# A two-block transformer kernel on one core: the layer mixers' projections issued in grains between recurrence and attention units, and GpSimd's remainder in four parts

## What is computed

```
h = h + 0.5 * swiglu(rmsnorm_2(h, ffn1_norm[l]), ...)
z = rmsnorm_2(h, mix_norm[l]) @ w_in[l]
(c_q, c_kv, k_pe, z_u, z_v, hq, hf, hi, hg, rq, rk, rv, rg) = jnp.split(z, split_points, axis=-1)
y_a = mla_mixer(c_q, c_kv, k_pe, ...)            # latent attention, 4 heads, causal softmax
y_b = spatial_gating_mixer(z_u, z_v, ...)        # gelu, layer norm, a 128x128 token mix per head
y_c = hgrn2_mixer(hq, hf, hi, hg, ...)           # gated linear recurrence, 4 heads of key width 128
y_d = retention_mixer(rq, rk, rv, rg, ...)       # decayed linear attention, 4 heads
h = h + jnp.concatenate([y_a, y_b, y_c, y_d], axis=-1) @ w_out[l]
h = h + 0.5 * swiglu(rmsnorm_2(h, ffn2_norm[l]), ...)
```

## Time and profile before

| | |
|---|---|
| median of 3 runs | 3614.14 us (3613.48 to 3615.37) |
| the profiled execution, its own time | 3615.54 us |
| its span, first to last instruction | 3614.2 us |
| mean granted TensorE clock | 0.947 of 2.4 GHz |
| TensorE busy | 3364.7 us, 93% |
| VectorE / GpSimd / ScalarE busy | 1723.3 / 1825.6 / 746.8 us |
| mixer of layer 0, first product of `cq` to first of `lout` | 1483.4 to 1887.2 us |
| mixer of layer 1, the same | 2723.4 to 3122.7 us |

### The profile page before, as it was taken

The page is one execution under the profiler, slowest core; times in us unless marked ns, Lnnn a source line. Parts: engine busy times, 40 slices in busy tenths (PEclk is TensorE's granted clock), DMA queues, the critical chain, the costliest instruction groups (busy, mean ns, idle before and its releaser), DMA issues.

```text
span 3614.2 us, 37344 instructions
## 1 busy us (share of the span) xinstructions
PE 3364.7 (93%) x14945; PEld 2647.4 (73%) x14945; DVE 1723.3 (48%) x2355; ACT 746.8 (21%) x1280; POOL 1825.6 (51%) x1024
## 2 busy tenths in 40 slices
PE   7989989899999999988669999999999886799998
PEld 4776567688888888866458888788887654688886
DVE  2333563378835851335575442454314356754314
ACT  3223223222212110222232110211002222211003
POOL 3334134477766666643006666666666320266665
PEclk9999689999999999999779999999999997899999
DMA  4211012133323333321003333233323210133332
GB/s 129 53 46 59 21 38 62 59 99 94 100 93 97 111 95 97 89 68 51 14 0 94 95 97 100 88 100 94 99 93 92 59 41 6 33 94 95 93 99 82
DMA packets 469285, 273.80 MB, mean 76 GB/s; under 512 B 20926, under 2 KB 466288, under 8 KB 468984
## 3 DMA queue, kind: packets, MB, share of 16 engines
q1 hardware_dynamic: 468056, 269.30, 25.3%
q10 hardware_dynamic: 1056, 2.12, 0.2%
HBM read 269.23 MB, written 2.12 MB: 75 GB/s over the span
## 4 chain that ended last, share of the span: by engine, by line
PE 87%; DVE 9%; ACT 2%; issue 1%; SPq 0%; POOL 0%; DMA 0%; DVEq 0%; ACTq 0%; POOLq 0%
PE bank L595 18%; PE bank L596 17%; PE bank L600 17%; PE bank L914 6%; PE bank L908 6%; PE bank L909 6%; DVE arena L1564 4%; PE bank L792 2%; PE bank L627 1%; PE bank L628 1%; PE bank L629 1%; PE bank L737 1%; PE bank L648 1%; PE bank L727 1%; PE bank L649 1%; PE bank L655 1%
## 5 line engine op out<-in xcount | busy, mean ns | idle before, releaser
L558 POOL TENSOR_SCALAR wh<-raw 128x1024 fp32r<-128x1024 f32 x510 | 565.9, 1110 | 1723.5 <-PE bank L600 963.2
L561 POOL TENSOR_TENSOR wl<-raw,wh 128x1024 fp32r<-128x1024 f32 x510 | 1260.8, 2472 | 42.6
L595 PE MATMUL bank<-xh,wh 128*128 128x512 f32 x1808 | 734.3, 406 | 0.0
L596 PE MATMUL bank<-xl,wh 128*128 128x512 f32 x1808 | 718.5, 397 | 0.0
L1564 DVE TENSOR_TENSOR arena<-arena 128x512 f32<-128x512 f32 (+3 forms) x514 | 535.8, 1062 | 64.3 <-ACT arena L1478 29.3
L600 PE MATMUL bank<-xh,wl 128*128 128x512 f32 x1808 | 446.6, 389 | 0.0
L595 PEld LDWEIGHTS bank<-xh,wh 128*128 128x128 f32 x1808 | 350.0, 194 | 80.8 <-issue 6.0
L596 PEld LDWEIGHTS bank<-xl,wh 128*128 128x128 f32 x1808 | 349.1, 193 | 77.2 <-issue 4.9
L600 PEld LDWEIGHTS bank<-xh,wl 128*128 128x128 f32 x1808 | 339.4, 188 | 70.6
L1564 DVE TENSOR_TENSOR arena<-bank,nrm 128x512 f32<-128x512 f32 x236 | 151.5, 683 | 386.2 <-PE bank L600 385.9
L595 PE MATMUL bank<-arena_rounded,wh 128*128 128x512 f32 x816 | 323.1, 396 | 0.0
(11 more groups left out here) (286 smaller groups left out, 4417.7 us busy)
## 6 DMA issues: line engine op xcount, KB each, us to landing
raw<-in_ffn_w_gate SPq DMA_DIRECT2D x176, 256.0 KB, 3.3
raw<-in_ffn_w_up SPq DMA_DIRECT2D x176, 256.0 KB, 3.2
raw<-in_ffn_w_down SPq DMA_DIRECT2D x176, 256.0 KB, 2.9
raw<-in_w_in SPq DMA_DIRECT2D x158, 256.0 KB, 3.3
raw<-in_w_up SPq DMA_DIRECT2D x88, 256.0 KB, 3.2
raw<-in_w_gate SPq DMA_DIRECT2D x64, 256.0 KB, 3.1
raw<-in_w_out SPq DMA_DIRECT2D x48, 256.0 KB, 3.1
raw<-in_w_down SPq DMA_DIRECT2D x44, 256.0 KB, 3.0
```

The costliest lines, as they stand in the source:

```text
L558: pool.tensor_scalar(wh[:, s, :], raw[:, s, :], 1.0, 0.0, ALU.mult, ALU.add).then_inc(split, 1)
L561: pool.tensor_tensor(wl[:, s, :], raw[:, s, :], wh[:, s, :].bitcast(F32), ALU.subtract).then_inc(split, 1)
L595: pe.matmul(psum, cols(wh, i), xhi, start=(i == 0), stop=False)
L596: pe.matmul(psum, cols(wh, i), xlo, start=False, stop=False)
```

## The change

Four things are changed together. (a) The projections of the mixers are issued as generators: `grains_fm` and `grains_tm` stop after every 8 products (16 narrow ones), and `fill(n)` issues the next n grains of a stream. (b) The mixer's order is new. First come `hf`, `hf`, `hq`; then the recurrence at once, in 32 units, with one or two grains of `hi`, `hq`, `cq`, `ckv`, `rq`, `rk`, `rv` behind each; then the latent products, the rotations and latent attention, with grains of `zu`, `zv`, `rg`, `hg` behind its units, and retention, its group norms and the spatial mix in fixed units of it. Tiles, banks, ScalarE's and VectorE's programs follow. SyncE loads the slabs in the new order, and loads the spatial weights behind a wait for the end of the recurrence. (c) Levels 64 and 32 are copied into `scT` by ScalarE, in one and two pieces without a mask, rather than by VectorE. `scT` is doubled. (d) GpSimd writes `wl` of every piece, in the whole kernel, in four instructions of 256 columns.

```diff
-MLA_BEHIND = ("zu", "zv", "rq", "rk", "rv")
+LOUT_ORDER = (4, 5, 6, 0, 2, 3, 7, 1)
+UNITS = NH * (len(LEVELS) + 1)
+UNIT_LEVELS = len(LEVELS) + 1
...
-            pool.tensor_tensor(wl[:, s, :], raw[:, s, :], wh[:, s, :].bitcast(F32), ALU.subtract).then_inc(split, 1)
+            for q in range(4):
+                c = slice(q * PIECE // 4, (q + 1) * PIECE // 4)
+                ins = pool.tensor_tensor(wl[:, s, c], raw[:, s, c], wh[:, s, c].bitcast(F32), ALU.subtract)
+            ins.then_inc(split, 1)
...
+        def grains_fm(key, rhs, ring=2):
+            s = slab_start(key, False, ring)
+            last = len(rhs) - 1
+            for b in range(2):
+                o, cols = bank[2 * s + b][:, :], piece_cols()
+                piece_split(1)
+                for i, (xhi, xlo) in enumerate(rhs):
+                    pe.matmul(o, cols(wh, i), xhi, start=(i == 0), stop=False)
+                    pe.matmul(o, cols(wh, i), xlo, start=False, stop=False)
+                    if i in (last // 2, last):
+                        yield
+                piece_split(2)
+                for i, (xhi, xlo) in enumerate(rhs):
+                    ins = pe.matmul(o, cols(wl, i), xhi, start=False, stop=(i == last))
+                piece_used(ins, *(("gemm", *key) if b else ("gemm0", *key)))
+                if b:
+                    done_at[key] = now[0]
+                yield "end" if b else None
...
-            gemm_fm(("cq", l), xk, f"lm{l}")
+            gemm_fm(("hf", 0, l), xk, f"lm{l}")
             squares(f"lm{l}", PT)
-            gemm_fm(("ckv", l), xk)
-            gemm_fm(("hf", 0, l), xk)
+            gemm_fm(("hf", 1, l), xk)
             rank_one(f"lm{l}")
-            norm(f"q{l}", [lprob[:, i, :] for i in range(2)], 1)
-            norm(f"kv{l}", [lprobT[:, 0, :]], 2)
-            gemm_fm(("hf", 1, l), xk)
             gemm_fm(("hq", 0, l), xk)
+            stream = itertools.chain(grains_tm(("hi", l), xk), grains_fm(("hq", 1, l), xk), grains_fm(("cq", l), xk),
+                                     grains_fm(("ckv", l), xk), grains_fm(("rq", l), xk), grains_fm(("rk", l), xk),
+                                     grains_tm(("rv", l), xk))
+            def fill(n):
+                for _ in range(n):
+                    if stop[0] != now[0] and next(stream, None) == "end" and narrow[0]:
+                        stop[0] = now[0]
+            stop, narrow = [None], [False]
...
+            for n in range(UNITS):
+                now[0] = n
+                hh, lv = divmod(n, UNIT_LEVELS)
+                level(n)
+                if lv in (1, 3):
+                    off_blocks(hh, lv // 2)
+                if lv == 2 and hh:
+                    recurrence_out(hh - 1)
+                if (hh, lv) == (2, 5):
+                    mean_square("h", 0, PT, gnt[:, 0, :])
+                if n == 23:
+                    slab_start(("qkv", l))
+                    norm(f"q{l}", [gnt[:, 1, :], qtmp], 1)
+                    norm(f"kv{l}", [nrm[:, 2, :]], 2)
+                fill(2 if n % 3 == 0 else 1)
+            now[0] = UNITS
+            fill(6)
+            assert done_at["rv", l] <= UNITS
...
+            recurrence_out(3)
...
+            for key in (("uk", l), ("uv", l)):
+                pe.wait_ge(*T.at("evac", *key))
+            narrow[0] = True
+            stream = itertools.chain(grains_fm(("zu", l), xk, 1), grains_tm(("zv", l), xk, 1),
+                                     grains_fm(("rg", l), xk, 1), grains_fm(("hg", l), xk, 1))
+            now[0] = -2
+            fill(1)
+            mean_square("h", 1, PT, gnt[:, 0, :])
...
+            now[0] = -1
...
+                fill(1 if n < 3 else 0)
...
+            def between(u):
+                now[0] = u
+                if u < 4 or 8 <= u < 12:
+                    a = 2 * u if u < 4 else 2 * u - 8
+                    for v in (a, a + 1):
+                        ret_score(v)
+                        fill(1)
+                        ret_out(v)
+                elif u in (4, 12):
+                    fill(1)
+                    mean(u // 8)
+                elif u in (6, 14):
+                    mean_square("r", u // 8, bank[2], gnr[:, 1, :])
+                    fill(1)
+                else:
+                    fill(2)
+                spatial(u)
...
+            turn[0] = 1
+            proj(f"lout{l}", xk, LOUT_ORDER, f"f2{l}")
...
+                if lv < len(LEVELS):
+                    act.wait_ge(*A.at("lvl_d", hh, lv, l))
+                    act.activation(hE[:, j % 2, :], hE[:, j % 2, :], ACT.Exp).then_inc(*A.up("lvl_e", hh, lv, l))
+                if lv in (1, 2):
+                    level_copy(n - 1)
+                if lv in (2, 4):
+                    act.wait_ge(*A.at("off", hh, lv // 4, l))
+                    if lv == 2 and hh:
+                        act.wait_ge(*A.at("hg_pv", hh - 1, l))
+                    a, b = (0, 512) if lv == 2 else (512, 768)
+                    act.activation(off[:, a:b], PT[:, 0:b - a], ACT.Copy).then_inc(*A.up("offs", hh, lv // 4, l))
...
+            rows_out(("hf", 0, l), hS[:, 0:2, :])
+            last()
+            v.memset(hQ, 0.0).then_inc(*V.up())
+            v.memset(hK, 0.0).then_inc(*V.up())
+            v.memset(scT, 0.0).then_inc(*V.up())
+            forget(0)
+            forget(1)
+            rows_out(("hf", 1, l), hS[:, 2:4, :])
+            sums(0)
+            tail(0)
+            sums(1)
+            forget(2)
+            forget(3)
+            sums(2)
+            sums(3)
+            rows_out(("hq", 0, l), hq[:, 0:2, :])
+            carried(0)
+            distances(0)
+            for n in range(UNITS):
+                hh, lv = divmod(n, UNIT_LEVELS)
+                if n + 1 < UNITS and (n + 1) % UNIT_LEVELS < len(LEVELS):
+                    distances(n + 1)
+                if lv < len(LEVELS):
+                    scaled_pair(n)
+                if n and (n - 1) % UNIT_LEVELS >= 2:
+                    masked(n - 1)
+                if lv == 3 and hh < NH - 1:
+                    tail(hh + 1)
+                if lv == 5 and hh < NH - 1:
+                    carried(hh + 1)
```

843 lines of the change are left out of this document (486 added, 357 removed).

## The result

The changed kernel takes 3554.67 us (median, 3553.47 to 3555.32), the kernel before in the same comparison 3614.76: a ratio of 0.983, 95% interval 0.9813 to 0.9847, 60 us or 1.7% less. The forecast was 3510 in a range of 3435 to 3580: the direction and the range held, the time lies above the 3465 to 3550 of the forecast's own case, and the gain came out at three fifths of the 104 us that the sum gave.

A forecast was written before the change was run, and what follows sets the result against it. VectorE was taken to bound the mixers' recurrence, leaving TensorE room for projections. A mixer's terms summed to 349.3 us against 401.5, 104.4 less in both layers: 3510 us, range 3435 to 3580.

The forecast's parts named there:

- the forecast's own case: Whole kernel: the summed forecast of 3510 us holds, own range 3465 to 3550, chance 0.56.
- A: Three slabs at the mixer's start (hf, hf, hq): as now, 34.3 us, from 34.6.
- C: Loop of 32 recurrence units: TensorE's 133 us bounds it by little, VectorE 124, 9 added in units 23 to 31: 142.
- D and E: Between loop and attention: latent products with ScalarE's copies 13 us, then rotations 38 (30 to 48).
- F, G, H: Attention 99 us (83 to 115), three low-clock restarts 6, wait before lout's third chunk 3.
- B: Wait for the first level, after the slabs: VectorE's queue outlasts TensorE's hq; 14 us, between 8 and 24.
- the port's 26: Loop: 14 pieces' remainders, 2.65 us each, stop VectorE about seven tenths of that, 26 us atop its own 98.
- Outside the mixers: First block and FFNs: a few us may come back, some pieces slow GpSimd; 0 taken, from -8 to +15.
- The remainder in four parts: GpSimd, every piece: four instructions take 2.65 us, a piece 3.8, hidden behind TensorE's 5.44.
- the fourth rival: Dense pieces: fixed instruction cost makes GpSimd the bound from 1.10 us a part; 3870 us at 1.3; chance 0.05.
- The first: Mixer loop: VectorE and the port bound it, loop 165 us, first-level wait 20, 3568 in all; chance 0.15.
- The third: Convolution: VectorE holds up each part, GpSimd takes 5.9 us a piece against 5.44; 3537 in all; chance 0.08.

The follow-up runs named there:

- late_cover: Kernel with all helpful edits combined, last slab's grains issued later in attention, its silu and gate two units later: 0.9691 of the kernel before.
- prefill: Changed kernel with the fourth slab's six grains ahead of the first level, 36 instead of 42 grains left in the loop: 0.9778 of the kernel before.
- after_1part: Changed kernel with the remainder in one instruction of 1024 columns instead of four: 3586.47 us, 0.991 of the kernel before.
- no_two_input: Changed kernel with the remainder not computed, GpSimd copying the piece with one input instead: 3484.67 us, 0.9623 of the kernel before.
- before_4parts: Kernel before the change with only the remainder split into four instructions: 1.0006 of the kernel before.

## Why the prediction was right, and where its sizes were wrong

**What bounds the kernel, and the direction.** Right. The mixers were where the room was; the recurrence was VectorE's, and projections fit beside it. The change gave 67 us in the mixers and lost 5 outside. That the order and not the parts made room is shown from both sides, 1.0006 with the parts alone and 0.991 with the order alone, but the sum gave all of the gain to the order: alone it gives half of it, and the other half needs both. The terms of a mixer missed by 2.3 (A), 5 (C), 2.6 (D and E) and 7.6 (F, G, H) us, all in the same direction; nothing cancelled. The time fell inside the range because the range reached to 3580, not because the sum was close.

**B, the wait for the first level: right.** 13.8 against 14, and with GpSimd out of the way 9.6, so the 5 us written for the port measured 4.2.

**C, the loop: 147.1 against 142.** TensorE's own work was 132.1 against the sum's 133.3. The idle time is 15.0 where 9 was written, and more than half of it not where: waits of 3.23, 1.84 and 2.03 us lie in the first two heads, in units 6, 12 and 14 (the first is unit 0). In units 23 to 31 are 5.9, most of it one wait for ScalarE's part of a norm, which the sum did not have and which is 2.9 us or more in every variant with the old number of grains, GpSimd's remainder or not:

```profile
2846.52 1.12 PE L762 MATMUL bank<-nrm,ones 128*128 128x512 f32 x2 [3.24 <-ACT nrm L1625]
```

The step that failed is "VectorE has 124 against 133, and TensorE bounds the loop by little", read as if the port's cost were hidden there. VectorE was in fact busy only 105.2 us, and 97.0 without the two-input instruction: its own work, with what GpSimd's other instructions hold up in it, is near the sum's 98, and the port's 26 was three times the 8 that this experiment takes away. Yet the idle time was larger than written. A total below the bound hides nothing at the units where VectorE's work bunches, and the longest of these waits, 3.23, is at the carried parts, which lie beside a piece. Without the two-input instruction the loop is 6.5 us shorter; with eight parts 7.

**A, the three slabs: 36.5 against 34.3.** The sum took them "as now". With one part they are 34.8, with no remainder 34.5: TensorE waits for the remainder, 1.71 us at the first slab, because the four parts take 4.46 us beside VectorE's two-input operations on the activations, where the kernel before's one part took 2.70 and VectorE did the waiting.

**D and E: 53.6 against 51** in layer 1, the pause in front of `zv` as forecast (8.31 against 8), the latent products 2 longer; in layer 0 they are 57.3, and TensorE is at the lower clock for part of them.

**F, G and H, attention: 115.6 against 108.** The largest single miss, and GpSimd is not its cause: 115.4 without the two-input instruction. The step that failed is the idle time: the sum carried over the old stage's (102.4 - 92.0 = 10.4), less 5 for pauses that grains fill, plus 3; measured is 115.6 - 97.7 = 18.0. VectorE's scaling ends 12.2 of it. That this chain is longer per unit because retention's scores, products with the decay and values are now in the same queues is likely and not shown; which part of the chain it is was not isolated. "From unit 10 nothing covers the chain" is right as a description; moving grains there did not help in late_cover, which moved the silu and the gate with them.

**Outside the mixers: +5 against 0.** Inside the written -8 to +15. The two effects have their sizes now: the first block gains 9.8 us, the FFNs and `lout` lose 14.8, of which one part gives back 7.5 and 4.1.

**The remainder in four parts: 2.79 us against 2.65.** By themselves one instruction takes 2.34 to 2.40, four take 2.79 to 2.84, eight 3.40: a further part costs 0.15 us, and the line through one and four holds at eight. So the fourth rival had its mechanism and nowhere near its size. The estimate from the 4497 ns that the Trainium skill's GPSIMD Engine Reference, Elementwise, states for 2048 columns, and from this trace's 2.40 for 1024, had been 3.3 for four parts; the row is lower. Beside VectorE the sum's 2.65 fails: four take 3.55, 4.18 and 4.46 us in the rows above.

**The rivals.** The first (VectorE and the port bound the loop, 3568) is nearer to the time than the forecast's own number, and its mechanism is there at single units, but prefill shows that TensorE's work still bounds the loop: with 11.3 us less of it the loop is 10.3 shorter. The loop's 147.1 and the wait's 13.8 are also far from that rival's 165 and 20, so its nearness to the time is luck. The third (the convolution becomes GpSimd's) did not come with four parts, by 0.2 us a piece, and came with eight. SBUF — State Buffer of the Trainium skill, Who interferes with whom, describes the lock as one for a whole instruction of whoever is first. The traces agree: halves of 0.42 us take 2.98 for two behind one part and the rounding after it, and GpSimd's four parts take 3.55 beside VectorE's work. By that rule two-input VectorE instructions take turns with the parts, as they do.

**What I said would show it.** Right: the clock row, the first level's delay, the pause in front of `zv`, VectorE's operations behind GpSimd well under 2 us (of the carried parts, two take 2.27), pieces 5.44 apart in the convolution. Wrong: that waits in the loop lie mainly in units 23 to 31. And both signs that were to prove the prediction wrong appeared, if small: pieces of an FFN are further apart where TensorE waits for the remainder (5.9 us of such waits between the mixers), and the level of the seventh unit was ready 3.23 us after its grain.

## What to carry to other kernels

An instruction that locks a port shared with another engine has no length of its own to optimise: its right size depends on who stands beside it. Here one part was best where TensorE waits for the remainder, four were better than one where VectorE's results are awaited in a chain (attention), and eight were best in the loop, where VectorE is dense and GpSimd has time to spare; where GpSimd itself is dense, in the convolution, eight cost 18 us. Choosing by stage was worth 0.9%, as much as the reordering by itself.

When work is moved beside other work, don't compare totals only; go through the units where the second engine's work bunches. And where TensorE is idle in front of a chain, first ask what it could issue there that needs nothing of the chain: the slab in the wait for the first level made each mixer 7 us shorter with three changed lines.

## What the runs showed of the hardware that was not expected

A short wait can cost several times its length through TensorE's clock. One part instead of four for two pieces made two waits 0.94 and 0.93 us longer, and the granted clock of the stage fell from 0.91 to 0.86 (between full speed, 2.4 GHz, and the lower level, 1.2 GHz): 5.9 us more busy time for the same products, 5.2 in the other layer. With one part everywhere it was 10.7 us.

VectorE's operations with a single input in SBUF were late beside GpSimd's remainder too: three of 128x128 (L1770) took 2.00 us at 2763.89 beside the parts; the same three in after_1part, with GpSimd idle, took 0.80:

```profile
2783.90 0.80 DVE L1767 TENSOR_SCALAR arena<-arena 128x128 f32<-128x128 f32 x3
```

GpSimd's one-input rounding holds up VectorE's two-input operations as well, as the row of no_two_input shows (1.64 for two halves that take 0.76 alone). Operations with one input in PSUM (the evacuations, the masked copies) did not get longer: the copies average 736 ns in the changed kernel's loop, and 727 in before_4parts, where GpSimd is idle beside them.
